# A two-layer decoder trunk on one core: the first layer's queries left unnormalised, their squares added to the outputs' squares

## The reference, cut to what matters

```python
def l2norm(x):
    xf = x.astype(jnp.float32)
    return xf * lax.rsqrt(jnp.sum(xf * xf, axis=-1, keepdims=True) + EPS)
...
    qkv = jax.nn.silu(causal_depthwise_conv(qkv, conv_w))
    ...
    q = l2norm(q) * (A_HEAD_DIM ** -0.5)
    k = l2norm(k)
    ...
    o = chunk_gated_delta_rule(q, k, v, g, beta)      # linear in q
    o = rmsnorm(o, o_norm) * jax.nn.silu(z)           # mean of o*o over the head's 128 dimensions, plus EPS
    return o @ w_out
```

## Time and profile before

| | us |
|---|---|
| three runs | 1352.55, 1352.83, 1353.82 |
| the profiled execution: its time | 1352.97 |
| its span, first to last instruction | 1351.2 |
| PE busy in it | 1295.7 (96%) |
| DVE busy | 972.5 (72%) |
| ACT busy | 683.4 (51%) |
| POOL busy | 561.1 (42%) |

### The profile page before, as it was taken

The page is one execution under the profiler, slowest core; times in us unless marked ns, Lnnn a source line. Parts: engine busy times, 40 slices in busy tenths (PEclk is TensorE's granted clock), DMA queues, the critical chain, the costliest instruction groups (busy, mean ns, idle before and its releaser), DMA issues.

```text
span 1351.2 us, 18103 instructions
## 1 busy us (share of the span) xinstructions
PE 1295.7 (96%) x6733; PEld 1051.1 (78%) x6733; DVE 972.5 (72%) x1687; ACT 683.4 (51%) x1082; POOL 561.1 (42%) x380
## 2 busy tenths in 40 slices
PE   7997999999999999999997999999999999998997
PEld 5786888888787878878885777777787878776786
DVE  5587888979898889885339757777777677777413
ACT  6355446364637364553226555656565555655303
POOL 6533333333333343432126693636456463632300
PEclk9998999999999999999999999999999999999999
DMA  7210110211111021115205111221111111218403
GB/s 193 76 46 16 32 48 16 64 31 48 48 46 49 16 63 32 59 37 213 82 32 187 32 32 33 67 65 56 48 48 47 47 48 47 62 48 296 172 0 125
DMA packets 106856, 91.40 MB, mean 68 GB/s; under 512 B 3105, under 2 KB 92306, under 8 KB 106770
## 3 DMA queue, kind: packets, MB, share of 16 engines
q1 hardware_dynamic: 106770, 90.25, 22.0%
HBM read 66.65 MB, written 23.59 MB: 67 GB/s over the span
## 4 chain that ended last, share of the span: by engine, by line
PE 72%; DVE 13%; ACT 7%; issue 7%; DMA 1%; POOL 0%; DVEq 0%; SPq 0%; ACTq 0%
PE psum L519 21%; PE psum L674 18%; PE psum L688 5%; PE psum L2486 4%; PE psum L2460 4%; PE psum L2473 2%; DVE terms L1904 2%; PE psum L2374 2%; PE psum L536 2%; DVE stick L2052 2%; PE psum L647 2%; PE psum L2285 1%; DVE small_L L1889 1%; PE psum L2358 1%; PE psum L2395 1%
## 5 line engine op out<-in xcount | busy, mean ns | idle before, releaser
L519 PE MATMUL psum<-u_hi,w_hi 128*128 128x512 f32 x640 | 260.4, 407 | 3.8 <-DVE u_lo L1616 1.7
L519 PE MATMUL psum<-u_hi,w_lo 128*128 128x512 f32 x640 | 258.9, 405 | 0.0
L519 PE MATMUL psum<-u_lo,w_hi 128*128 128x512 f32 x640 | 257.8, 403 | 0.0
L486 POOL TENSOR_TENSOR w_lo<-w_raw,w_hi 128x1024 fp32r<-128x1024 f32 (+1 forms) x45 | 108.4, 2410 | 237.4 <-ACT w_hi L481 225.6
L519 PEld LDWEIGHTS psum<-u_hi,w_hi 128*128 128x128 f32 x640 | 120.8, 189 | 29.7 <-issue 4.3
L519 PEld LDWEIGHTS psum<-u_hi,w_lo 128*128 128x128 f32 x640 | 120.9, 189 | 24.0 <-issue 1.9
L519 PEld LDWEIGHTS psum<-u_lo,w_hi 128*128 128x128 f32 x640 | 121.1, 189 | 20.9 <-issue 0.5
L1759 DVE SCALAR_TENSOR_TENSOR late<-raw,cols,late 128x1024 f32<-128x1024 f32 x72 | 130.2, 1808 | 1.8
L616 POOL TENSOR_TENSOR w_lo<-w_raw_b,w_hi 128x512 fp32r<-128x512 f32 x40 | 52.7, 1319 | 136.8 <-ACT w_hi L600 136.8
L2052 DVE TENSOR_TENSOR_SCAN stick<-soft 128x1024 f32<-128x1024 f32 (+3 forms) x64 | 103.7, 1620 | 0.2
L481 ACT ACTIVATE w_hi<-w_raw 128x1024 fp32r<-128x1024 f32 (+1 forms) x45 | 45.9, 1020 | 109.5 <-PE psum L519 109.3
(11 more groups left out here) (300 smaller groups left out, 3201.2 us busy)
## 6 DMA issues: line engine op xcount, KB each, us to landing
...
```

The lines of the kernel that those rows point to most:

```text
L486: G.tensor_tensor(lo_tiles(key), raw_tiles(key), hi_tiles(key).bitcast(F32), ALU.subtract).then_inc(lo_done, 1)
L519: mm = PE.matmul(psum[:, half], (w_hi, w_hi, w_lo)[part][:, buffer(key), k], (u_hi, u_lo, u_hi)[part][:, k, half * HALF:(half + 1) * HALF] ...
```

## The change: what it does, and the diff

- The queries are no longer normalised. Their squares are not summed by PE, there is no Ln, Exp or product for them; `L2374` reads the silu's result `conv[:, 0]` and so does the product with the decay (L1923 before, L1957 after). `Xs`, `sq_lo_q` and half of `sq_hi` are gone; the rows of the inverse get a small tensor of their own.
- In their place ScalarE squares the queries once more with a scale of P*sqrt(EPS), half by half (`square_q`, slots 5 and 13 of the head's preparation), and VectorE adds that to the outputs' squares (`add_q`), so that the sum carries EPS times c*c. The rest of EPS stands in the bias `eps_o`.
- The outputs' squares are summed in two fp32r parts: the upper part on ScalarE (`upper_o`), the lower on VectorE (`lower_o`), both in `sq_hi`. The sum of the second half moves from slot 0 to the end of slot 1 and from bank 2 to bank 5.
- The copy of the outputs out of PSUM moves from VectorE to ScalarE, behind `square_o`.
- The table load behind the squares now stands at the end of slot 21, behind the keys' squares.
- Two semaphores for parameters are merged into one.

```diff
+        sq_hi = sb("sq_hi", [P, T], F32R, delta_mem)
+        q_sq_first = sd("q_sq_first", [P, HALF])
+        q_sq_second = sd("q_sq_second", [P, 2, HALF])
...
-            def square_kq(h, n):
+            def square_k(h):
                 if h > 0:
                     for g in range(2):
-                        if n == 0:
-                            lb_done[g].wait(act, h - 1, LEVELS)
-                        else:
-                            inv_mm[g].wait(act, h - 1, INV_MM)
-                silu_kq.wait(act, h, turn_of(h, n) + 1)
-                A.activation(sq_kq[n], conv[:, 1 - n], ACT.Square).then_inc(sq_ready.handle, 1)
-                sq_ready.wait(act, h, turn_of(h, n) + 1)
-                A.activation(sq_hi[:, n], sq_kq[n], ACT.Copy).then_inc(sq_hi_done.handle, 1)
-                if turn_of(h, n) == 1:
-                    A.preload_act_table_set(LN_EXP)
+                        lb_done[g].wait(act, h - 1, LEVELS)
+                silu_kq.wait(act, h, 2)
+                A.activation(sq_k, conv[:, 1], ACT.Square).then_inc(sq_ready.handle, 1)
+                sq_ready.wait(act, h, 1)
+                A.activation(sq_hi[:, :], sq_k, ACT.Copy).then_inc(sq_hi_done.handle, 1)
+                A.preload_act_table_set(LN_EXP)
+
+            def square_q(h, half):
+
...
+                    if h > 0:
+                        o_split.wait(act, h - 1, O_ADDED)
+                elif h > 1:
+                    o_split.wait(act, h - 2, 3 + O_ADDED)
+                silu_kq.wait(act, h, 2)
+                A.activation(q_sq_first[:, :] if half == 0 else q_sq_second[:, h % 2], conv[:, 0, half_range(half)],
+                             ACT.Square, scale=P * sqrt(EPS)).then_inc(q_sq_done.handle, 1)
 
...
                 osum_ready.wait(act, t, half + 1)
-                A.activation(o_rs[:, :], psum[:, 5 if half == 0 else 2], ACT.Ln, bias=eps_d[:, 0:1], scale=1.0 / P
+                A.activation(o_rs[:, :], psum[:, SUM_BANK], ACT.Ln, bias=eps_o[:, 0:1], scale=1.0 / P
...
+                if half == 1:
+                    og_done.wait(act, t, 1)
+                elif t > 0:
+                    og_done.wait(act, t - 1, 2)
+                A.activation(o_nrm[:, :], psum[:, 3], ACT.Copy, scale=cols[:, ONORM_COL:ONORM_COL + 1]
+                             ).then_inc(o_copied.handle, 1)
+
+            def upper_o(t, half):
+                o_split.wait(act, t, 3 * half + O_ADDED)
+                A.activation(o_sq_hi, o_sq[:, :], ACT.Copy).then_inc(o_split.handle, 1)
 
...
+                if s == 13:
+                    upper_o(t, 0)
...
+                    sums_ready.wait(act, h, 1)
+                    A.activation(rs_k, banks(4), ACT.Ln, bias=eps_d[:, 0:1]).then_inc(ln_done.handle, 1)
                 if s == 1:
-                    for n in range(2):
-                        ln_done.wait(act, h, n + 1)
-                        A.activation(rs_kq[n], rs_kq[n], ACT.Exp, scale=-0.5,
-                                     bias=(0.0, q_scale[:, 0:1])[n]).then_inc(rs_ready.handle, 1)
+                    ln_done.wait(act, h, 1)
+                    A.activation(rs_k, rs_k, ACT.Exp, scale=-0.5).then_inc(rs_ready.handle, 1)
+                if s == 5:
+                    square_q(h, 1)
+                if s == 13:
+                    square_q(h, 0)
                 if s == 2:
...
-                    if s == 0 and t >= 1:
+                    if s == 2 and t >= 1:
                         norm_scale(t - 1, 1)
...
+                    if s == 0 and t >= 1:
+                        upper_o(t - 1, 1)
...
-                    if s in (21, 22) and t + 2 < H:
-                        square_kq(t + 2, s - 21)
+                    if s == 21 and t + 2 < H:
+                        square_k(t + 2)
...
+            upper_o(H - 1, 1)
...
                         if s == 2:
                             tok_ready.wait(dve, h - 1, 4)
+                        elif s == 1:
+                            norm_done.wait(dve, h - 1, 1)
+                            sq_ready.wait(dve, h - 1, 1)
                         else:
-                            norm_done.wait(dve, h - 1, 2)
-                            sq_ready.wait(dve, h - 1, 2)
+                            qg_done.wait(dve, h - 1, 1)
...
 
-            def copy_o(t, half):
+            def add_q(t, half):
+
                 osq_done.wait(dve, t, half + 1)
-                V.tensor_scalar(o_nrm[:, :], psum[:, 3], cols[:, ONORM_COL:ONORM_COL + 1], None, ALU.mult
-                                ).then_inc(o_copied.handle, 1)
+                q_sq_done.wait(dve, t, 2)
+                V.tensor_tensor(o_sq[:, :], o_sq[:, :], q_sq_first[:, :] if half == 0 else q_sq_second[:, t % 2], ALU.add
+                                ).then_inc(o_split.handle, 1)
+
+            def lower_o(t, half):
+                o_split.wait(dve, t, 3 * half + O_HI)
+                V.tensor_tensor(o_sq_lo, o_sq[:, :], o_sq_hi.bitcast(F32), ALU.subtract).then_inc(o_split.handle, 1)
 
...
-                    for n, (dst, part_no) in enumerate(((kT, 1), (qT, 0))):
-                        rs_ready.wait(dve, h, n + 1)
-                        V.tensor_tensor(flat(dst[:, c]), conv[:, part_no], rs_kq[n], ALU.mult
-                                        ).then_inc(norm_done.handle, 1)
+                    rs_ready.wait(dve, h, 1)
+                    V.tensor_tensor(flat(kT[:, c]), conv[:, 1], rs_k, ALU.mult).then_inc(norm_done.handle, 1)
...
+                    if h > 0:
+                        lower_o(h - 1, 0)
                     tokens(h, 0)
...
+                    if s == 12 and t == H - 1:
+                        lower_o(t, 0)
                     if s == 0 and t >= 1:
-                        copy_o(t - 1, 1)
+                        add_q(t - 1, 1)
                     if t + 1 < H:
                         prepare(t + 1, s)
+                    if s == 1 and t >= 1:
+                        lower_o(t - 1, 1)
...
-            copy_o(H - 1, 1)
+            add_q(H - 1, 1)
             for i in range(2):
                 add_output(i, LAST_GROUP + i, 16 * (KB - HOME))
+                if i == 0:
+                    lower_o(H - 1, 1)
...
             def sum_squares_o(t, half):
-                osq_done.wait(pe, t, half + 1)
-                PE.matmul(psum[:, 5 if half == 0 else 2], ones[:, :], o_sq[:, :], start=True, stop=True
-                          ).then_inc(osum_ready.handle, 1)
+                o_split.wait(pe, t, 3 * half + O_LO)
+                for i, part in enumerate((o_sq_hi, o_sq_lo)):
+                    mm = PE.matmul(psum[:, SUM_BANK], ones_r[:, :], part, start=i == 0, stop=i == 1)
+                mm.then_inc(osum_ready.handle, 1)
...
-                        if t > 0:
-                            oln_done.wait(pe, t - 1, 2)
...
-                    for n in range(2):
-                        if n == 1 and t >= 1:
-
-                            sum_squares_o(t - 1, 1)
...
                     sum_in.wait(pe, h, 2)
-                    ln_done.wait(pe, h, 2)
+                    ln_done.wait(pe, h, 1)
...
                 if s == 4:
-                    norm_done.wait(pe, h, 2)
...
                             dec_ready.wait(pe, h, 3)
-                        for src, bk in ((kT, (6, 4)[half]), (qT, (7, 5)[half])):
...
-            sum_squares_o(H - 1, 1)
+                    if s == 1 and t >= 1:
+                        if t + 1 < H:
+                            ln_done.wait(pe, t + 1, 1)
+                        sum_squares_o(t - 1, 1)
             for i in range(2 * KB):
                 last_group(i)
+                if i == 1:
+                    sum_squares_o(H - 1, 1)
```

109 lines of the change are left out of this document (55 added, 54 removed).

## The result

The changed kernel takes 1366.2 us in the median of four runs (1364.39 to 1367.08), the kernel before 1352.69 in its four; the ratio is 1.0099, with a 95% interval from 1.0087 to 1.0111. It is 13.5 us slower. I had forecast 1359.3 with a range up to 1363.5: the direction and the places were right, the size was half of what came, and the time lies outside the range.

The account below looks back on a forecast made before the run. PE was taken as the bound, with only 2.0 us idle a pass. 6 x 0.37 + 6 x 0.7 = +6.4, -2.9 and +3.0 gave +6.5 on 1352.97: 1359.5, as median 1359.3; range 1349.8 to 1363.5.

Parts of the forecast that it names:

- The single events: Effects outside the six passes: -2.9 at the layer's start, +0.3 and -0.4 in pass 6, +1.1 in pass 7, +2.0 after the last head.
- The wait for `lower_o`: Behind slot 1, GpSimd blocks DVE's tap, so PE waits 1.24 plus 0.11 refill, then 0.46 for the sum.
- The table load ahead of `v_new`: End of a pass: the 1.28 us load delays `v_new`, so PE stalls 1.29 at L2320, six times.
- Slot 13: Later packing and `k_tail` make the sum end 0.5 later, the next packing 0.2: +0.7 a pass, bounds 0 and +1.2.
- Slot 13 of pass 7: No transposes between, so the chain `v_new`, `upper_o`, `lower_o` is 1.5 late, minus 0.41: +1.1.
- the sums that PE no longer makes at slot 0: Before slot 0's projections, the outputs' sum with its wait and the queries' sums go: -2.73 a pass.
- the start of the layer: Queries' sums go at t = -1, -0.93, and PE's waits for DVE shrink in t = 0, -1.98: together -2.9.
- the tail: After the last head the sum comes two groups later and `lower_o` meets GpSimd: +2.0, or 0.85 without the block.
- the load does delay PE: Against the rival that the table load does not delay PE: 6 x 1.29 less, 1351.6; chance 0.06.
- the block does fall in slot 1: Against the rival of no block in slot 1: -9.3, 1350.0; chance 0.12.
- slot 13 is not hidden: Against the rival that slot 13 is mostly hidden by unseen slack on DVE and ACT: 1355; chance 0.12.
- rival 5: DVE becomes the bound if its 1.4 us of slot 13 don't come back: 0.7 more a pass, 1364; chance 0.08.

Follow-up runs that it names:

- e2: Changed kernel with ScalarE's split of the weight block ending in slot 23, and GpSimd's subtraction behind it, two slots later (passes 0 to 5); 1354.58 us.
- e6: Changed kernel with `lower_o` of the second half moved on DVE from behind both taps to between them; 1357.49 us.
- e1: Changed kernel with the table load of passes -1 to 5 put back behind `v_new` of slot 22; 1358.60 us.
- e4: Kernel before the change, with only the table load in slots 21 and 22 moved ahead of `v_new`; 1358.08 us, ratio 1.0037 to before.
- e5: Changed kernel with the queries' Square of slot 13 put behind ScalarE's packing of `inv_first`; 1364.72 us.

## Why the prediction was wrong

The profiled execution is 4.9 us above the worked-out 1359.5, and 5.5 of that are in the six passes, six times 1.98 - 1.07. The single events outside them came out at -0.1 together (11.75 - 6 x 1.98) where I had +0.1 (-2.9 + 0.3 - 0.4 + 1.1 + 2.0), and what follows layer 0 is 0.3 shorter.

*The wait for `lower_o`: mechanism right, size off; this is the step that failed.* I had +1.81 for the wait, its refill and the sum, it was +2.34: 3.2 of the 5.5 us. I wrote that DVE "does the first tap by 431.7, then starts the first SCALAR_TENSOR_TENSOR", beside GpSimd's start at 430.8, and let the block fall on the second. What I took for free was the TENSOR_SCALAR. It was held for 2.2 us, until 0.5 behind GpSimd, and then the second tap took its whole 1.28: `lower_o` could start 1.8 behind GpSimd's end, not 1.08. GpSimd, now the first of the two, took 2.41 and not 2.69, which gave 0.3 of that back. PE's wait came to 1.66 (forecast 1.24) and its refill to 0.22 (forecast 0.11). e2 and e6 show both halves of this. My own numbers had GpSimd starting (430.8) ahead of the tap (which I had from 430.95), where before the tap came first, DVE's timeline of the kernel before against 430.91 of the earlier trace rows:

```profile
430.59 0.74 DVE L1756 TENSOR_SCALAR late<-raw,cols 128x1024 f32<-128x1024 f32 x1
```

I used the row's 3.31 without asking which instruction would be in front in the new order. The Trainium skill (SBUF — State Buffer, SBUF: two separate sides) has it: the lock is also taken by a DVE instruction "in a 2-port perf mode", and who starts first keeps it. This tap has one SBUF input and goes through 1024 columns in 0.74, where an instruction with two takes 1.28. I had quoted the half of the rule on two inputs only. The trace agrees with both halves; that this tap runs in such a mode I take from its 0.74.

*The table load ahead of `v_new`.* Forecast +1.29, measured +1.51, 1.3 us in all. The load is 1.28, and taking it back gave 1.27 (e1). The other 0.2 is a part of the change that I read over. The keys' Square waited for the first of the two silus (`turn_of`), now it waits for both (`silu_kq.wait(act, h, 2)`), that is for the instruction right ahead of it on its own engine. Before, the Square starts 1.92 behind the silus, after, 2.12 (ScalarE's timelines, before and then after):

```profile
421.58 2.01 ACT L1317 ACTIVATE late<-late 128x1024 f32<-128x1024 f32 x2
423.50 1.04 ACT L1309 ACTIVATE dec<-late 128x1024 f32<-128x1024 f32 x1
```

```profile
424.56 2.01 ACT L1328 ACTIVATE late<-late 128x1024 f32<-128x1024 f32 x2
426.68 1.06 ACT L1310 ACTIVATE dec<-late 128x1024 f32<-128x1024 f32 x1
```

`v_new` stands behind the Square. The 0.2 doesn't go with the table load: e1 has the new wait and the load behind `v_new`, its Square starts 2.12 behind in all seven heads, and from slot 22 to L2320's place PE still takes 2.95 instead of 2.73; e4 has the old wait and the load ahead, its Square starts 1.91 behind in all seven, and the same stretch takes 4.02, only the load's 1.29 more. That it is the wait, and not something else of the change that e1 shares, is read from rows; no kernel was run with the wait alone changed.

*Slot 13.* +0.52 and +0.31 against +0.5 and +0.2, 0.8 us in all. The prediction had two chains late here, ScalarE's packing and DVE's `k_tail`, and took its +0.5 from the second, the sum that starts when `k_tail` is done. That held: e5 takes the packing's delay away and nothing moves, since `lower_o` still delays `k_tail` by as much. (What I wrote ahead of e5, that the 0.5 was the packing's, was not what the prediction says.) Of two chains that are late together, taking one away wins nothing, whichever has its name in the wait.

*The single events*, too, are off one by one, and that their sum is right is luck. Slot 13 of pass 7 came at +1.9 where I had +1.1: PE waits 2.11 there for `lower_o`. Pass 6 and the missing cost of slot 16 in pass 0 give -0.9 where I had -0.1.

*What went right.* The -2.72 for the sums that PE no longer makes at slot 0 and the start of the layer (-3.3, forecast -2.9); the tail's +2.2 (norm's product 8.92 behind the last L2359 instead of 6.72; forecast +2.0). The rivals' mechanisms did not come: the load does delay PE, the block does fall in slot 1, slot 13 is not hidden. The number of rival 5, 1364, was nearer than mine, but not its reason: DVE is busy for 63.8 of 75.8 and PE's waits end with other things.

*The last 1.9 us*: the median, 1366.2, is 1.8 above the profiled execution, 1364.39; in the kernel before it had been 0.14 below it. The eight runs of this kernel go with the mean granted clock: at 0.995 and 0.996 they took 1364.1 to 1364.8, at 0.994 1366.0 and 1366.3, at 0.992 and 0.993 1366.4 to 1367.2. I had not allowed for this; the range ended 0.9 below even the fastest of the first four.
